# A transformer layer with 32 experts: the weight ring of four pairs becomes three thirds, with its chunks fetched ahead moved to experts 14 to 17

## What is computed

```python
n2 = rms_norm(h, norm2_w, NORM_EPS).reshape(B * S, D_MODEL)
logits = n2 @ w_router + b_router            # top 4 of 32, softmax over the four
gu = xb @ w_gu[e] + b_gu[e]                  # 1024 x 2048 for each expert
act = gate * sigmoid(1.702 * gate) * (up + 1)   # gate, up clamped at 7
y = act @ w_down[e] + b_down[e]              # 1024 x 1024 for each expert
h = h + segment_sum(y * gw)
```

## Time and profile before

| | us |
|---|---|
| median of 3 runs (988.66 to 989.54) | 988.99 |
| the profiled execution | 988.7 |
| its span, first to last instruction | 986.9 |
| PE busy, share of the span | 946.6 (96%) |
| DVE, ACT, POOL busy | 202.9, 127.7, 14.0 |
| mean granted clock of TensorE | 0.987 |
| moved from HBM | 416.80 MB (here 1 MB is 10^6 bytes), 423 GB/s over the span |

### The profile page before, as it was taken

How to read it: one execution, slowest core, us unless ns; L and a number is a source line. 1 busy time by engine, 2 the same in 40 slices (tenths; PEclk the granted TensorE clock), 3 DMA queues, 4 the chain that set the end, 5 groups by cost and what they waited for, 6 DMA issues and landing times.

```text
span 986.9 us, 11112 instructions
## 1 busy us (share of the span) xinstructions
PE 946.6 (96%) x4508; PEld 382.4 (39%) x4508; DVE 202.9 (21%) x610; ACT 127.7 (13%) x346; POOL 14.0 (1%) x9
## 2 busy tenths in 40 slices
PE   9999999999999899898989989889989999999997
PEld 5545433333333334333333333333333333333432
DVE  4645121212111121210112121011212112111121
ACT  2433111011110111010011101001101110011101
POOL 0031000000000000000000000000000000000000
PEclk9999999999999999999999999999999999999999
DMA  9999999999999999999999999999999999999996
GB/s 374 426 423 398 412 429 434 432 430 428 432 431 429 436 430 430 434 432 429 434 433 426 437 432 428 437 430 429 436 429 431 432 429 430 431 433 430 422 422 272
DMA packets 23869, 418.27 MB, mean 424 GB/s; under 512 B 2912, under 2 KB 3296, under 8 KB 8224
## 3 DMA queue, kind: packets, MB, share of 16 engines
q1 hardware_dynamic: 23408, 417.20, 99.2%
q10 hardware_dynamic: 432, 0.66, 0.2%
HBM read 416.80 MB, written 1.05 MB: 423 GB/s over the span
## 4 chain that ended last, share of the span: by engine, by line
PE 63%; DMA 36%; DVE 1%; issue 0%; ACT 0%; SPq 0%; DVEq 0%
DMA ring<-w_gu_dram 33%; PE ps L1237 29%; PE ps L1342 14%; PE ps L1205 4%; PE ps L1189 4%; DMA ring<-w_down_dram 3%; PE ps L1066 3%; PE ps L997 2%; PE ps L1004 1%; PE ps L1293 1%; PE ps L1301 1%; PE ps L1013 0%; PE ps L1039 0%; PE ps L1058 0%; PE ps L1046 0%
## 5 line engine op out<-in xcount | busy, mean ns | idle before, releaser
L1237 PE MATMUL ps<-ring,passing 128*64 128x512 f32 x1008 | 229.1, 604 | 14.8 <-DMA ring<-w_gu_dram 14.8
L1237 PE MATMUL ps<-ring,PR 128*64 128x512 f32 x976 | 224.5, 608 | 16.4 <-DMA ring<-w_gu_dram 16.2
L1342 PE MATMUL ps<-ring,PT 128*64 128x512 f32 x984 | 218.3, 595 | 0.5 <-DMA ring<-w_down_dram 0.5
L952 DVE TENSOR_SCALAR xw<-ps 128x256 f32<-128x256 f32 x64 | 27.2, 425 | 650.0 <-PE ps L1237 650.0
L1237 PEld LDWEIGHTS ps<-ring,passing 128*64 128x64 f32 x1008 | 76.8, 139 | 158.3 <-issue 143.8
L1237 PEld LDWEIGHTS ps<-ring,PR 128*64 128x64 f32 x976 | 74.9, 140 | 157.0 <-issue 145.4
L1342 PEld LDWEIGHTS ps<-ring,PT 128*64 128x64 f32 x984 | 68.1, 137 | 129.6 <-issue 127.5
L652 ACT ACTIVATE xw<-xw 128x256 f32<-128x256 f32 x64 | 26.6, 416 | 484.5 <-DVE xw L952 484.5
L1205 PE MATMUL ps<-PT 64*128 64x512 f32 x248 | 69.7, 640 | 0.0
L1189 PEld LDWEIGHTS ps<-qk,X 128*128 128x128 f32 x512 | 59.6, 191 | 18.8 <-issue 18.8
L1189 PE MATMUL ps<-qk,X 128*128 128x128 f32 x512 | 65.7, 281 | 0.0
(11 more groups left out here) (198 smaller groups left out, 374.6 us busy)
## 6 DMA issues: line engine op xcount, KB each, us to landing
ring<-w_gu_dram SPq DMA_DIRECT2D x48, 4096.0 KB, 28.2
ring<-w_down_dram SPq DMA_DIRECT2D x25, 4096.0 KB, 29.7
ring<-w_gu_dram SPq DMA_DIRECT2D x14, 2048.0 KB, 14.2
ring<-w_gu_dram SPq DMA_DIRECT2D x6, 3072.0 KB, 23.2
ring<-w_down_dram SPq DMA_DIRECT2D x5, 2048.0 KB, 23.1
ring<-w_gu_dram SPq DMA_DIRECT2D x9, 1024.0 KB, 9.6
ring<-w_down_dram SPq DMA_DIRECT2D x8, 1024.0 KB, 25.9
ring<-w_down_dram SPq DMA_DIRECT2D x2, 3584.0 KB, 27.6
```

The source lines that it names most:

```text
L952: nc.vector.tensor_scalar(gb[:, b, :], gu[:, b, 0, :], LIMIT, None, ALU.min).then_inc(g_ready, 1)
L1237: last = mm(ps[64 * j:64 * j + 64, GU + b, :], lhs, halves[j][:, 512 * b:512 * b + 512], start=start, stop=stop)
L1342: last = mm(ps[64 * j:64 * j + 64, bank, :], at[:, k, 64 * (c - GU_PIECES):64 * (c - GU_PIECES) + 64], rows[:, 512 * j:512 * j + 512], sta ...
```

## The change

The ring becomes nine pieces, three *thirds* (parts) of 6 MB, 48 KB to a partition; the place for the ninth piece is that of `extra`. w_gu and w_down become one tensor, `w_all`, in which half an expert (three pieces) lies together: part 2e holds gate-and-up pieces 0 to 2 of expert e, part 2e + 1 its piece 3 and the down pieces. One load brings a part, from part 10 (expert 5) to part 52 (first half of expert 26), and SP waits until all three old pieces of the third are used. Up to piece 29 (experts 0 to 4) loads are pieces of 2 MB, and so they are from piece 159 to 179 (second half of expert 26 to expert 29), with semaphores of their own (`landed_late`). Experts 30 and 31 keep their cuts, except that the last chunk (512 KB) comes in two column halves, whose matmuls PE does one after the other; ACT copies the result in two halves, and the last sums over the tokens are made by halves too.

Chunks fetched ahead are now the first of experts 14 to 17 (eight loads of 512 KB, the same eight blocks) and the first of part 29 of expert 14 (`later_ahead`, two loads). The four loads into `extra`, the first ones after the first ring pieces, are gone; one piece of 2 MB, piece 8, is loaded in that place. The loops of PE and of SP over the experts are gone: experts 1 to 29 are written out one by one. The bias product of the down projection (L1378) comes after expert 5 instead of after expert 3.

```diff
-RING = 8
+RING = 9
...
-LAST_TWO = [(2, c) for c in range(GU_PIECES)] + [(3, c) for c in range(GU_PIECES)] + [(u, c) for u in (2, 3) for c in range(GU_PIECES, PIECES)]
 PIECE = 4096
-PAIR = 2 * PIECE
-FIRST_FILL = (1, 2, 2, 3)
-BY_CHUNK, SINGLES = (RING, RING + 1, RING + 3), 14
-MORE_LANDINGS, LATER_LANDINGS = (3, 1, 3, 1), (1, 1, 1, 0)
-END_CUTS = {(2, 2): ((4, 6), (6, 8)), (3, 0): ((0, 2), (2, 4)), (3, 2): ((4, 6), (6, 7), (7, 8)),
-            (2, 4): ((0, 2), (2, 4), (4, 6), (6, 7), (7, 8)), (3, 4): ((0, 2), (2, 4), (4, 6), (6, 7), (7, 8))}
+PART = 3
+TRIPLE = PART * PIECE
+SLOTS_OF = RING // PART
+HALVES = NE * 2
+FIRST_PLACE = (NE - 2) * PIECES
+LAST_TWO = [(e, c) for e in (NE - 2, NE - 1) for c in range(GU_PIECES)] + [(e, c) for e in (NE - 2, NE - 1) for c in range(GU_PIECES, PIECES)]
+BY_CHUNK, SINGLES = (RING, RING + 1, RING + 3), 21
+LANDINGS = (2, 3, 4, 4, 6, 3, 3, 3, 3, 3)
+LATE = 2 * (NE - 6) + 1
+END_CUTS = {(NE - 2, 0): ((0, 4),), (NE - 2, 2): ((4, 6), (6, 8)), (NE - 1, 0): ((0, 2), (2, 4)), (NE - 1, 2): ((4, 6), (6, 7), (7, 8)),
+            (NE - 2, 4): ((0, 2), (2, 4), (4, 6), (6, 7), (7, 8)), (NE - 1, 4): ((0, 2), (2, 4), (4, 6), (6, 7))}
+LAST_COLUMNS = ((0, 256), (256, 512))
 X_CUTS, W_CUTS = ((0, 1), (1, 2), (2, 4), (4, 8)), ((0, 1), (1, 2), (2, 3), (3, 4), (4, 6), (6, 8))
 H_CUTS = (((0, 512), (512, 1024)), ((0, 512), (512, 896), (896, 1024)))
...
+AHEAD, AHEAD_FROM = 4, 14
...
-        "w_down": w_down.reshape(NE, 8, P, DM).transpose(0, 2, 1, 3).reshape(NE, P, PAIR),
+        "w_all": np.concatenate([w_gu.reshape(NE, 8, P, 2, 2, 2, FF // 4).transpose(0, 2, 1, 4, 5, 3, 6).reshape(NE, P, GU_PIECES * PIECE),
+                                 w_down.reshape(NE, 8, P, DM).transpose(0, 2, 1, 3).reshape(NE, P, (PIECES - GU_PIECES) * PIECE)],
+                                2).reshape(NE, P, 2, TRIPLE).transpose(0, 2, 1, 3).reshape(HALVES, P, TRIPLE),
     }
...
-        extra = sb("extra", [P, 4, 1024])
...
-            def load(slot, row, src, first, stop):
-
-                dst = ring[:, slot * PIECE + first:slot * PIECE + stop].rearrange("p (o n) -> p o n", o=1)
-                return sp.dma_start(dst, src[:, bass.ds(row, 1), first + slot % 2 * PIECE:stop + slot % 2 * PIECE])
...
+            def load(part, slot, first=0, stop=TRIPLE, at=None):
+
+                at = slot * TRIPLE + first if at is None else at
+                dst = ring[:, at:at + stop - first].rearrange("p (o n) -> p o n", o=1)
+                return sp.dma_start(dst, w_k[:, bass.ds(part, 1), first:stop])
+
+            def load_piece(s, first=0, stop=PIECE, done=None):
+
+                part, base = s // PART, s % PART * PIECE
+                load(part, part % SLOTS_OF, base + first, base + stop).then_inc(done or landed[part % SLOTS_OF], 16)
+
+            def load_part(part, skip):
+
+                load(part, part % SLOTS_OF, skip).then_inc(landed[part % SLOTS_OF], 16)
...
             def load_ahead(n):
 
-                src = w_gu_k[:, (NE - 2 * TURN + n // 2) * 2, 0:2 * FF]
-                sp.dma_start(ahead[n], src[:, n % 2 * FF:(n % 2 + 1) * FF]).then_inc(ld_ahead[n // 2], 16)
-
-            def load_down_ahead(u):
-
-                sp.dma_start(down_ahead[u], w_dn_k[:, NE - 2 * TURN + u, 0:DM]).then_inc(ld_down_ahead[u], 16)
+                sp.dma_start(ahead[n], w_k[:, 2 * (AHEAD_FROM + n // 2), n % 2 * FF:(n % 2 + 1) * FF]).then_inc(ld_ahead[n // 2], 16)
+
+            def load_later_ahead(j):
+
+                sp.dma_start(later_ahead[j], w_k[:, 2 * AHEAD_FROM + 1, j * FF:(j + 1) * FF]).then_inc(ld_later_ahead[j], 16)
...
-            load_pair(0)
+            load_piece(0, stop=2 * PIECE)
             load_piece(RING + 2)
-            for n in range(8, 2 * AHEAD):
-                load_ahead(n)
+            load_piece(RING - 1)
...
@@ -472,34 +475,40 @@
             for s in range(RING + 5, RING + SINGLES):
                 sp.wait_ge(pieces_used, s + 1 - RING)
                 load_piece(s)
-            for s in range(RING + SINGLES, RING + 2 + TP, 2):
-                sp.wait_ge(pieces_used, s + 2 - RING)
-                load_pair(s)
-            with sp.Fori(1, TURNS - 3) as r:
-                for s in range(RING + 2, RING + 2 + TP, 2):
-                    sp.wait_ge(pieces_used, r * TP + s + 2 - RING)
-                    load_pair(s, r * TURN)
-            for s in range(RING + 2, 3 * TP - 2 * PIECES, 2):
-                sp.wait_ge(pieces_used, (TURNS - 3) * TP + s + 2 - RING)
-                gu_ahead = 0 <= s - TP < AHEAD * PIECES and s % PIECES == 0
-                load_pair(s, NE - 3 * TURN, 2 * FF if gu_ahead else DM if s in (TP + GU_PIECES, TP + PIECES + GU_PIECES) else 0)
+            first_part = (RING + SINGLES) // PART
+            for part in range(first_part, LATE):
+                sp.wait_ge(pieces_used, PART * (part + 1) - RING)
+                begun = 0 <= part // 2 - AHEAD_FROM < AHEAD and part % 2 == 0 or part == 2 * AHEAD_FROM + 1
+                load_part(part, 2 * FF if begun else 0)
+            for s in range(PART * LATE, FIRST_PLACE):
+                sp.wait_ge(pieces_used, s + 1 - RING)
+                load_piece(s, done=landed_late[s % RING])
             for n in range(0, 2 * PIECES, 2):
-                u, c = LAST_TWO[n]
-                s = 3 * TP - 2 * PIECES + n
-                sp.wait_ge(pieces_used, (TURNS - 3) * TP + s + 2 - RING)
...
-                    for k, stop in END_CUTS[u, c]:
...
+                if (e, first_c) == (NE - 1, GU_PIECES):
+                    part, first, at = place_of(KC - 1)
+                    ends = ring[:, at:at + DM].rearrange("p (j n) -> p j n", j=2)
+                    rows = w_k[:, part, first:first + DM].rearrange("p (j n) -> p j n", j=2)
+                    for q, (a, b) in enumerate(LAST_COLUMNS):
+                        sp.dma_start(ends[:, :, a:b], rows[:, :, a:b]).then_inc(landed_cols[q], 16)
...
+            act.wait_ge(pieces_used, NE * PIECES)
+            for done, (a, b) in zip((y_first, y_sb), LAST_COLUMNS):
+                nc.scalar.copy(ye_last[:, a:b], ps[:, GU + 1, a:b]).then_inc(done, 1)
 
...
                 def wait_landed(c):
-                    s = place(c)
-                    pair = s % RING // 2
-                    fills = FIRST_FILL[pair] + s // RING
-
-                    if not (isinstance(turn, int) and turn == 0) or s >= RING:
-                        fills += MORE_LANDINGS[pair]
-                    if not (isinstance(turn, int) and turn == 0) or s >= 2 * RING:
-                        fills += LATER_LANDINGS[pair]
+                    part = 2 * e + c // PART
+                    if part >= LATE:
+                        s = e * PIECES + c
+                        pe.wait_ge(landed_late[s % RING], 16 * ((s - PART * LATE) // RING + 1))
+                        return
+                    if c % PART > 0:
+                        return
...
+                    fills = sum(LANDINGS[m] if m < len(LANDINGS) else 1 for m in range(part % SLOTS_OF, part + 1, SLOTS_OF))
+                    pe.wait_ge(landed[part % SLOTS_OF], 16 * fills)
...
+                        if late and k == 0:
                             wait_landed(c)
...
+                        in_columns = step == "last" and c == PIECES - 1 and k == 3
+                        for q, (a, b) in enumerate(LAST_COLUMNS if in_columns else ((0, 512),)):
+                            if in_columns:
+                                pe.wait_ge(landed_cols[q], 16)
+                            for j in range(2):
+                                last = mm(ps[64 * j:64 * j + 64, bank, a:b], at[:, k, 64 * (c - GU_PIECES):64 * (c - GU_PIECES) + 64],
+                                          rows[:, 512 * j + a:512 * j + b],
+                                          start=c == GU_PIECES and k == 0, stop=c == PIECES - 1 and k >= (2 if step == "last" else 3), skip_group_check=in_columns)
...
-                    pe.wait_ge(GdT_sb, 1)
-                expert(0, u, "first" if u == 0 else None)
-
-            pe.wait_ge(ld_bdn, 16)
+            expert(0, "first")
             pe.wait_ge(GdT_sb, 1)
-            for t in range(T):
-                for c in range(2):
-                    mm(ps[:, ACC[t] + c, :], GdT[c * NE:(c + 1) * NE, t, :], bdn[c * NE:(c + 1) * NE, :], start=False, stop=True, skip_group_check=True)
-            with pe.Fori(1, TURNS - 2) as r:
-                for u in range(TURN):
-                    expert(r, u)
-            for u in range(TURN):
-                expert(TURNS - 2, u, early=u)
-
-            for u in range(TURN - 2):
-                expert(TURNS - 1, u, early=TURN + u)
-            gate_up, between, _, _, down = expert(TURNS - 1, TURN - 2, "last but one")
+            for e in range(1, NE - 2):
+                expert(e, early=e - AHEAD_FROM if 0 <= e - AHEAD_FROM < AHEAD else None)
+                if e == TURN + 1:
+                    pe.wait_ge(ld_bdn, 16)
+                    for t in range(T):
```

(51 more changed lines are left out.)

99 lines of the change are left out of this document (39 added, 60 removed).

## The result

| | before | changed |
|---|---|---|
| median, us (range, runs) | 989.21 (988.66 to 989.54, 7) | 992.95 (991.61 to 994.49, 7) |
| the profiled execution | 988.7 | 994.49 |
| its span | 986.9 | 992.6 |
| packets of the instruction queue q8 | 21 | 38 |

The change makes the kernel slower by 3.7 us: ratio 1.0038, interval 1.0028 to 1.0047. Run again beside other kernels it took 992.20 (991.86 to 992.35, 6 runs) where the kernel before took 989.03, a ratio of 1.003 [1.0018, 1.0043]. The 13 runs have a median of 992.28 and fall into two heaps, ten from 991.61 to 992.95 and three from 993.69 to 994.49; the profile shown here (the *first trace*) is of the slowest one. A *second trace* is of an execution of 992.28 us. Lines for L1237, L1342 and L1205 of before are now L1249, L1357 and L1216.

What follows compares the result with a forecast made beforehand. The prediction took the stream of weights, plus PE's work and output after its last landing, as the bound. Terms -0.7 + 0.2 + 2.1 + 0 - 0.3 = +1.3 us gave a median of 990.3, range 987.3 to 993.2.

Steps and rivals of the forecast that it cites:

- rival 1: Experts 8 to 23: each code packet delays the slowest queue, 0.2 us each, 3.4 us in all, 991.6; chance 0.24.
- With more packets the hits spread more evenly, so I take the middle, +2.1 us: Unrolled experts: 17 more code packets hit the 16 DMA engines, between 0.7 us (even sharing) and 3.4 us.
- The two stretches: Profile of before, 776.64 to 882.11 and 882.11 to 928.65 us: time beyond the loads', read as 0.2 to 0.25 a packet.
- Fewer loads, -0.7: Whole weight stream: 10 loads fewer at 0.07 us each save 0.7 us, bounds -0.5 and -1.0.
- Rows of 48 KB, 0: Triples, 253 MB: rows of 48 KB move as those of 32 KB, so 0 us.
- Rival 3: Triples: longer rows stream better by 3 GB/s, saving 4.3 us, 986.0; chance 0.11.
- rival 5: Triples: the hardware cuts them into pieces, so they save none of the 0.7 us, 991.0; chance 0.04.
- The early chunks moved, 0: Experts 14 to 17 and 24 to 29: moving early chunks only shifts PE's waits and drops no bytes, 0 us.
- The switch to triples, 0: After expert 3: part 10 begins to land 1.1 us before the queue runs dry, so 0 us.
- Rival 4: Switch to triples: the queue runs dry, costing up to 1 us, 991.3; chance 0.04.
- The tail, -0.3: Kernel end: with column halves the first half's matmuls finish before the second lands, -0.3 us, bounds -0.5 and 0.
- the 1-KB rows, +0.2: Last chunk's column halves: 1 KB rows where 4 KB stood load slower, +0.2 us, between none and 0.3.

Runs made afterwards that it cites:

- the 86 loads: The changed kernel with every 6 MB third from expert 5 on loaded as three 2 MB pieces, 86 loads more: 998.18 us.
- the first group: The first of three groups of follow-up runs; the kernel before, unaltered, took 989.29 us in it (988.47 to 990.34, 16 runs).
- 9 blocks on POOL: The kernel before with 2304 one-element memsets written out on POOL, 9 blocks of 256 instructions: 996.00 us, ratio 1.0072.

## Why the prediction was right and wrong

The range (987.3 to 993.2) held the 992.95. The likeliest case, no change at 990.3, did not come; slower did, 3.7 us, for the greater part (2.84) by the mechanism of rival 1.

- **The bound, and what costs**: right. The stream of weights is the bound, full but for the end, and PE's own order has no price.
- **38 packets, 16 of them in mid-kernel**: right.
- **"With more packets the hits spread more evenly, so I take the middle, +2.1 us"**: this step failed. Written out alone, the loop costs 2.84 us, 0.17 a packet, exactly the point from which rival 1 was to decide. The hits do not even out over 16 engines: eight end 5.9 to 7.6 us behind the fastest, and seven within 4.0. Each hit on the slowest adds to the lag, and little takes it off again while the queue is full. The two stretches that gave 0.2 to 0.25 were nearer than the middle, 0.12; halving them had no row behind it.
- **Fewer loads, -0.7**: 0.07 us a load is confirmed in size by the 86 loads (0.06 to 0.07). That the ten fewer loads here gave 0.6 back is not seen: the fastest engine is done at 974.10 in the second trace, and at 973.55 in the kernel before written out, which has the ten loads more.
- **Rows of 48 KB, 0**: right, 14.53 us a triple. Rival 3 falls, as does rival 5 (38 loads of 6144 KB and five of 5120 KB stand in the page).
- **The early chunks moved, 0**: not always. The prediction set them against PE's waits in experts 15 to 17 and left out that expert 14 has 2 MB ahead. Together the four need 43 MB, 104.4 us of stream, against PE's 105.0, so a late PE stays late there. In the first trace it came 3.3 us late and the stream lost 2.2 us; in the second none.
- **The switch to triples, 0**: right; SP issues at once, and in the second trace nothing is lost there. In the first trace a load near the switch lands 1.4 us later than in the second one (216.93 for 215.50) with the fastest engine no later (213.25 for 213.59); a code packet starts at 214.7, and the lag grows from 2.35 to 3.68. Rival 4 did not come.
- **The tail, -0.3, and the 1-KB rows, +0.2**: no gain. PE saves 0.1 us behind the last landing, and the last store's issue takes longer (1.59 us for 0.70); with the old tail put back the median is 0.4 us lower rather than higher, within the intervals. The step missed that PE may not wait for the last load at all, and that the stores come behind it. What the 1-KB rows cost by themselves no run shows.

The sum with what was measured: 2.84 - 0.6 + 0 to 0.4 = 2.2 to 2.6, where 3.2 and 3.7 were seen. **About 1 us stays open.** The traces point to two parts of it: the 0.6 of the fewer loads, which does not show, and the loss at experts 14 to 17, which takes 2.2 us of the first trace and nothing of the second. Whether that loss is what parts the two heaps of runs no run tells. The rest is scatter by engine: four packets from 195 to 305 us take the lag from 1.7 to 2.4 in the kernel before, and from 2.4 to 3.6 in the first trace of the changed one. On which engine a packet falls no row tells. The runs of the changed kernel spread over 2.9 us, the first seven of before over 0.9 and the 16 of the first group over 1.9.

## What to carry to other kernels

In this kernel, which streams weights without a gap, a load is as late as its slowest DMA engine, and that lag adds up to the end. So count what else those engines carry: code that is written out instead of looped is fetched once, 16 KB a packet on PE, at 0.17 us each here, and code on an idle engine was no cheaper (0.40 to 0.57 us per 8 KB). An unrolled loop must earn that. And what is fetched ahead should be spread so that no expert needs less of the stream than PE's own time: where four in a row need no more, a PE that once came 3.3 us late had no wait left to make it up in.

## What the runs showed that was not expected

- A lag between DMA engines stays, to hundredths of a microsecond, for over 400 us, until another packet changes it (2.44 at 274, 2.46 at 685 us), as it would if the queue is never empty for the fast ones. It did shrink where they ran dry (the first trace, at 490 us) and, a little, at other places (11.79 to 11.53 us from 215 to 274 us, with 9 blocks on POOL).
- POOL's 128 instructions make a packet of 8 KB, where PE's packets have 16 KB. The Trainium skill, Advanced Engine Details and Errata, section ISA Cache, gives lines of 16 KB; PE's q8 agrees (38 packets, 0.62 MB), POOL's q14 does not (42 packets, 0.34 MB).
- Nineteen microseconds can be lost to 0.28 MB of fetched code that does nothing, on an engine that nobody waits for, because one DMA engine carries all of it.
- A wait of PE can cost more than itself: in one of 3.9 us the granted clock fell to half for 6.8 us, and 20 matmuls took 7.10 us for 4.09.
